# Gathering the tokens of two experts with one set of products, and moving a put into the next expert's chunks

## The chip, the cores and the metric

One core of a Trainium2 chip runs the whole program. Its engines are TensorE (PE, whose weight loads have rows of their own, PEld), VectorE (DVE), ScalarE (ACT), GpSimd (POOL) and SyncE (SP, which issues the weight transfers here). They run side by side and meet at semaphores. The metric is the device time of one execution in microseconds (us); of several runs the median counts.

## The reference

The kernel computes one inference step of a two-layer decoder for 320 tokens (a prompt of 256, and 8 sequences of 8 new tokens), 1024 features each, in float32. Each layer has a mixer (three kinds of recurrent heads) and a feed-forward part. The first layer's feed-forward part is dense. The second layer's is a mixture: a router picks 2 of 8 experts for each token, and each expert is a SwiGLU of width 1408.

```python
def moe_swiglu(h, router, wg, wu, wd):
    probs = softmax(h @ router)
    top_p, top_i = lax.top_k(probs, TOP_K)            # TOP_K = 2
    top_p = top_p / jnp.sum(top_p, axis=-1, keepdims=True)
    gates = jnp.sum(one_hot(top_i, N_EXPERTS) * top_p[..., None], axis=-2)
    out = jnp.zeros_like(h)
    for e in range(N_EXPERTS):                        # N_EXPERTS = 8
        out = out + gates[..., e:e + 1] * swiglu(h, wg[e], wu[e], wd[e])
    return out
...
def swiglu(h, wg, wu, wd):
    return (jax.nn.silu(h @ wg) * (h @ wu)) @ wd
```

After it come x += out and a final RMSNorm.

## The kernel before, in words

**Layout.** Activations are held feature by feature: `x` is 8 tiles of 128 features by 320 tokens. Each float32 operand of a large product is split into a high and a low part (`hh` and `hl`, `whi` and `wlo`), and a product is made as three: high by high, high by low, low by high.

**Weights.** All weights come as a stream of slots, each 128 x 1024 numbers (512 KB). SP loads a slot into one of 11 places of `wraw`, as soon as PE has used the slot eleven before (semaphore `slot_used`). ACT copies it, rounded, into one of 3 places of `whi` (L1196) when PE has used the slot three before; DVE subtracts to get `wlo` (L1630); then PE may use it (`slot_split`). An expert has 33 slots: 22 for gate and up, in six chunks (five of 4 slots and 512-column products, one of 2 slots and 256-column products), and 11 for down.

**One expert (layer 2, when no expert has more than 128 tokens).** The loop over the eight experts is a hardware loop (`Fori`) on each engine; the order in it is fixed by hand for each engine, and the engines wait for each other's counts.

- *Gather.* The tokens of expert i are collected by products with a 0/1 matrix: `pick` (made by DVE in `picks`, L2083) has a 1 where a token takes a place. `htk` holds the token rows, high and low part. `gather` (L1065) makes 8 feature tiles x 3 token blocks x 2 parts = 48 products of 128 columns, into banks 6 and 7 (high) and 2 and 3 (low). ACT copies the high banks into `hh` (L1526), DVE the low ones into `hl` (L2175).
- *Scales.* `slot_scales` (L1074) makes three small products that give each place its token's gate and norm factor; ACT copies them into `slot_g` (L1534).
- *Gate and up.* For each chunk PE makes 24 products (L1108 to L1110) with the places stationary and the weights moving. ACT makes `sil` (L1557), DVE `hid` (L2199), and two slots into the next chunk PE turns `hid` over (`turn`, L1092); ACT and DVE split it into `hidh` and `hidl`.
- *Placement.* `pick` is transposed by PE (L1118), and DVE copies it to `place` (L2203).
- *Down.* 66 products of 512 columns (L1129) into banks 4 and 5. ACT scales the result by the gate (`gated`, L1544), DVE makes its low part (L2192, semaphore `y_lo`).
- *Next gather.* Directly behind the last down product stand the gather and the scales of expert i + 1 (also behind expert 7, for a ninth that doesn't exist: the tables have nine columns for it).
- *Put.* 16 products of 320 columns (L1147, L1148) spread the result over the tokens, 8 feature tiles into banks 4 to 7 in turn. Even tiles go by ACT (`yt`, L1568) and POOL (L2411, x += yt); odd ones are added to `x` by DVE (L2215). Tile 4 waits for ACT's copy of tile 0 (`put_free`), tile 5 for DVE's addition of tile 1 (`dn_free`), and so on.

On DVE the order at a slot is: low part of the slot three ahead, then the chunk's `hid` if a chunk ends there, then the others. On ACT it is the high part of the slot three ahead, then silu. At slot 32 both do the part of y first.

The first gather, for expert 0, stands ahead of the loop. After the loop ACT squares `x` for the last norm (L1212), when POOL and DVE have made all their additions.

Of the kernel before, what the change touches and what calls it, by code (L numbers as in the profile page):

```python
# [22 lines left out]
F32 = mybir.dt.float32  # L23
F32R = mybir.dt.float32r
ALU = mybir.AluOpType
# [208 lines left out]
def trunk(nc, x_in, w_in, consts_in, par_in, s_rw, s_rt, s_mb, s_sh, s_cv,  # L234
# [4 lines left out]
    with ctx:  # L239
# [127 lines left out]
        pos9 = sb("pos9", [P, 3, NEXP + 1])  # L367
        rt1 = sb("rt1", [P, 3, 4])
        rs_tok = sb("rs_tok", [P, 3])
        gate_rs = sb("gate_rs", [P, 3, 2, NEXP + 1])  # L370
        slot_g = sb("slot_g", [P, 2])
# [5 lines left out]
        pick = sb("pick", [P, 3, P], F32R)  # L377
# [116 lines left out]
        def _(pe):  # L494
# [565 lines left out]
            def gather():  # L1060

                for z, bk in enumerate((6, 2)):
                    for k in range(KT):
                        for q in range(3):
                            m = mm(B[bk + k // 4][:, (k % 4) * P:(k % 4 + 1) * P], htk[z][:, q, k * P:(k + 1) * P],  # L1065
                                   pick[:, q, :], start=(q == 0), stop=(q == 2))
                    m.then_inc(S("taken"), 1)

            def slot_scales(i):

                for q in range(3):
                    of = gate_rs[:, q, :, i] if isinstance(i, int) else \
                        gate_rs[:, q, :, bass.ds(i, 1)].rearrange("p a o -> p (a o)")
                    m = mm(B[1][:, 256:258], pick[:, q, :].bitcast(F32), of,  # L1074
                           start=(q == 0), stop=(q == 2))
                m.then_inc(S("taken"), 1)

            def experts_picked():
# [3 lines left out]
                gather()  # L1082
# [12 lines left out]
                def body(i, g, e):  # L1095
                    pe.wait_ge(S("taken_hi"), 2 * i + 1)
                    pe.wait_ge(S("taken_lo"), i + 1)

                    for c, (j0, nj, nf) in enumerate(CHUNKS):
                        if c == 1:  # L1100
                            pe.wait_ge(S("taken_hi"), 2 * i + 2)
                        for j in range(j0, j0 + nj):
                            r = G_FFN[L] + j
                            pe.wait_ge(S("slot_split"), g + j + 1)
                            for kk in range(KT // nj):
                                k, cols = (j - j0) * (KT // nj) + kk, slice(kk * 2 * nf * P, (kk + 1) * 2 * nf * P)
                                out = B[c % 2][:, 0:2 * nf * P]
                                mm(out, hh[:, k, 0:P], whi[:, r % HI, cols], start=(k == 0), stop=False)  # L1108
                                mm(out, hl[:, k, 0:P], whi[:, r % HI, cols], start=False, stop=False)  # L1109
                                m = mm(out, hh[:, k, 0:P], wlo[:, POS[r], cols], start=False, stop=(k == KT - 1))  # L1110
                            m.then_inc(S("slot_used"), 1)
                            if j in TURN:
                                turn(i, TURN[j])

                    pe.wait_ge(S("put_free"), i * 4 + 4)
                    pe.wait_ge(S("dn_free"), i * 4 + KT * (1 + N_E[0]))
                    for q, (c0, n) in enumerate(BLOCKS):
                        m = pe.transpose(B[6][:, c0:c0 + n], pick[0:n, q, :].bitcast(F32),  # L1118
                                         C("ident", 0, n, slice(0, n)))
                    m.then_inc(S("place_pe"), 1)  # L1120
                    for f in range(FT):
                        if f % 2 == 0:
                            pe.wait_ge(S("hid_split"), i * NC + (N_E[0] * FT + f // 2 + 1))
                        pe.wait_ge(S("slot_split"), g + 2 * FT + f + 1)
# [9 lines left out]
                    pe.wait_ge(S("place_in"), 2 * i + 2)  # L1134
                    gather()
# [52 lines left out]
        def _(act):  # L1188
# [333 lines left out]
            def taken_hi(i):  # L1522

                act.wait_ge(S("taken"), 3 * i + 1)
                for z in range(2):
                    m = af(hh[:, 4 * z:4 * z + 4, 0:P], bank(6 + z, 4, P), ACT.Copy)  # L1526
                m.then_inc(S("taken_hi"), 1)

            def slot_scales(i):

                act.wait_ge(S("taken"), 3 * i + 3)
                if not isinstance(i, int):
                    act.wait_ge(S("y_lo"), 2 * i)
                af(slot_g[:, :], B[1][:, 256:258], ACT.Copy).then_inc(S("taken_hi"), 1)  # L1534

            def experts_picked():
# [3 lines left out]
                def gated(i, g):  # L1540

                    act.wait_ge(S("slot_used"), g + EXP_SLOTS)
                    for z in range(2):
                        af(hidh[:, 4 * z:4 * z + 4, P:2 * P], bank(4 + z, 4, P), ACT.Copy,  # L1544
                           scale=slot_g[:, 0:1]).then_inc(S("y_hi"), 1)

                def body(i, g, e):
                    for j in range(EXP_SLOTS):
                        if j == EXP_SLOTS - 1:
                            gated(i, g)  # L1550
# [989 lines left out]
```

## Time and profile before

| | |
|---|---|
| median of 3 runs | 1612.6 us (1605.84 to 1612.98) |
| the profiled execution | 1610.96 us; span in the trace 1609.2 us |
| busy over the span | PE 1449.9 us (90%), DVE 919.8 (57%), ACT 755.6 (47%), POOL 128.8 (8%) |
| mean granted clock of TensorE | 0.879 of full speed |
| weight stream | 217.61 MB over queue q1, 39.8% of the 16 DMA engines |

The span goes from the first to the last instruction of the trace. The experts run from about 1110 to 1591 us. "Granted clock" is 1.00 at 2.4 GHz and 0.50 at 1.2 GHz; a mean between them is a mixture of stretches at either level. Starts and durations of PE rows are modelled at their ends: products overlap, so the pace is read from one start to the next.

### The profile page before, as it was taken

To read this page: it belongs to the slowest core of one execution; us is meant where nothing else is said; L and a number is where in the kernel's file an instruction comes from. 1 tells how busy PE (TensorE), PEld (TensorE's weight loads), DVE (VectorE), ACT (ScalarE), POOL (GpSimd) and SP (SyncE) were. 2 spreads that over 40 slices of the span, in tenths; PEclk is the share of its full clock that TensorE was granted. 3 is DMA by queue.
4 is the path that set the end of the run, shared out by engine and by line. 5 is a ranking of instruction groups with operands and counts; after the bars stand their busy time and mean duration, and the time that the engine had idled before them with its cause. 6 is when DMAs were issued, how large, how long until landed. Compare 5 with 4: busy or idle time off the path is not lost.

```text
span 1609.2 us, 27125 instructions
## 1 busy us (share of the span) xinstructions
PE 1449.9 (90%) x10509; PEld 1253.4 (78%) x10509; DVE 919.8 (57%) x1443; ACT 755.6 (47%) x1130; POOL 128.8 (8%) x162
## 2 busy tenths in 40 slices
PE   5897889896999999889788889879999999999996
PEld 4886777766999999878667777678788778878875
DVE  4634443425554554455454343353888888988885
ACT  5521322303443243363223240344877777777784
POOL 1111011100000000001111101100000000000000
PEclk8987886856999999999778685687999999999998
DMA  5311211012554544132121110151977977977881
GB/s 222 103 63 46 67 51 58 2 51 78 199 154 132 155 146 136 49 115 79 54 73 40 42 41 8 61 204 54 326 280 278 339 277 282 340 273 273 330 291 69
DMA packets 62207, 234.93 MB, mean 146 GB/s; under 512 B 7073, under 2 KB 7169, under 8 KB 61345
## 3 DMA queue, kind: packets, MB, share of 16 engines
q1 hardware_dynamic: 59472, 217.61, 39.8%
q0 software_dynamic: 2496, 13.71, 2.3%
q10 hardware_dynamic: 144, 2.28, 0.3%
q8 instruction: 69, 1.13, 0.3%
q14 instruction: 26, 0.20, 0.0%
HBM read 225.48 MB, written 8.09 MB: 145 GB/s over the span
## 4 chain that ended last, share of the span: by engine, by line
PE 67%; issue 18%; DVE 7%; ACT 5%; POOL 1%; DMA 0%; ACTq 0%; POOLq 0%; DVEq 0%
PE bank L504 11%; PE bank L505 10%; PE bank L506 10%; PE bank L498 7%; PE bank L1129 4%; PE bank L1108 2%; PE bank L1110 2%; PE bank L1109 2%; PE bank L1065 2%; ACT whi L1196 2%; PE bank L626 1%; PE bank L520 1%; PE bank L644 1%; DVE wlo L1630 1%; PE bank L658 1%
## 5 line engine op out<-in xcount | busy, mean ns | idle before, releaser
L1630 DVE TENSOR_TENSOR wlo<-wraw,whi 128x1024 fp32r<-128x1024 f32 x410 | 506.2, 1238 | 310.4 <-ACT whi L1196 304.3
L1196 ACT ACTIVATE whi<-wraw 128x1024 fp32r<-128x1024 f32 x410 | 433.2, 1059 | 364.0 <-PE bank L506 280.0
L504 PE MATMUL bank<-hh,whi 128*128 128x320 f32 x608 | 220.2, 362 | 33.4 <-DVE hl L1654 13.8
L505 PE MATMUL bank<-hl,whi 128*128 128x320 f32 x608 | 207.8, 342 | 0.0
L506 PE MATMUL bank<-hh,wlo 128*128 128x320 f32 x608 | 206.6, 340 | 0.0
L504 PEld LDWEIGHTS bank<-hh,whi 128*128 128x128 f32 x608 | 133.3, 219 | 48.8 <-issue 31.5
L1108 PE MATMUL bank<-whi,hh 128*128 128x512 f32 (+1 forms) x384 | 149.0, 388 | 0.8 <-DVE hl L2175 0.3
L1110 PE MATMUL bank<-wlo,hh 128*128 128x512 f32 (+1 forms) x384 | 144.5, 376 | 0.0
L1109 PE MATMUL bank<-whi,hl 128*128 128x512 f32 (+1 forms) x384 | 144.1, 375 | 0.0
L505 PEld LDWEIGHTS bank<-hl,whi 128*128 128x128 f32 x608 | 133.7, 220 | 0.4
L506 PEld LDWEIGHTS bank<-hh,wlo 128*128 128x128 f32 x608 | 132.1, 217 | 0.0
L504 PE MATMUL bank<-rawh,whi 128*128 128x320 f32 x352 | 108.7, 309 | 0.0
L506 PE MATMUL bank<-rawh,wlo 128*128 128x320 f32 x352 | 108.2, 308 | 0.0
L505 PE MATMUL bank<-rawl,whi 128*128 128x320 f32 x352 | 108.2, 308 | 0.0
L1108 PEld LDWEIGHTS bank<-whi,hh 128*128 128x128 f32 x384 | 73.0, 190 | 19.5 <-DVE wlo L1630 2.8
L1110 PEld LDWEIGHTS bank<-wlo,hh 128*128 128x128 f32 x384 | 72.9, 190 | 13.7
L1109 PEld LDWEIGHTS bank<-whi,hl 128*128 128x128 f32 x384 | 73.2, 191 | 10.4
L2411 POOL TENSOR_TENSOR x<-x,yt 128x320 f32<-128x320 f32 x32 | 27.1, 881 | 508.8 <-ACT yt L1568 508.8
L504 PEld LDWEIGHTS bank<-rawh,whi 128*128 128x128 f32 x352 | 66.0, 187 | 0.2
L505 PEld LDWEIGHTS bank<-rawl,whi 128*128 128x128 f32 x352 | 66.0, 187 | 0.2
L506 PEld LDWEIGHTS bank<-rawh,wlo 128*128 128x128 f32 x352 | 66.0, 187 | 0.0
L504 PE MATMUL bank<-hidh,whi 128*128 128x320 f32 x184 | 60.2, 327 | 4.0 <-DVE hidl L2106 4.0
(388 smaller groups left out, 2454.3 us busy)
## 6 DMA issues: line engine op xcount, KB each, us to landing
wraw<-in_w SPq DMA_DIRECT2D x410, 512.0 KB, 4.9
smb<-in_s_ssm POOLq DMA_DIRECT2D x2, 1536.0 KB, 6.9
out_o_ssm<-smb POOLq DMA_DIRECT2D x2, 1536.0 KB, 5.4
cst<-in_consts ACTq DMA_DIRECT2D x1, 2225.0 KB, 13.0
srw<-in_s_rwkv POOLq DMA_DIRECT2D x2, 768.0 KB, 4.4
out_o_rwkv<-srw POOLq DMA_DIRECT2D x2, 768.0 KB, 3.6
x<-in_x SPq DMA_DIRECT2D x1, 1280.0 KB, 5.7
out_y<-x SPq DMA_DIRECT2D x2, 640.0 KB, 3.0
```

What stands on the lines that cost most here:

```text
L498: return pe.matmul(out, lhsT, rhs, start=start, stop=stop, skip_group_check=True)
L504: mm(out, hi, rh, start=first, stop=False)
L505: mm(out, hi, rl, start=False, stop=False)
L506: return mm(out, lo, rh, start=False, stop=last)
L1065: m = mm(B[bk + k // 4][:, (k % 4) * P:(k % 4 + 1) * P], htk[z][:, q, k * P:(k + 1) * P], pick[:, q, :], start=(q == 0), stop=(q == 2))
L1108: mm(out, hh[:, k, 0:P], whi[:, r % HI, cols], start=(k == 0), stop=False)
L1109: mm(out, hl[:, k, 0:P], whi[:, r % HI, cols], start=False, stop=False)
L1110: m = mm(out, hh[:, k, 0:P], wlo[:, POS[r], cols], start=False, stop=(k == KT - 1))
L1129: m = mm(B[4 + z][:, :], h_[:, f, 0:P], w_[:, z * 512:(z + 1) * 512], start=(f == 0 and q == 0), stop=(f == FT - 1 and q == 2))
L1196: af(whi[:, ring % HI, :], wraw[:, POS[ring], :], ACT.Copy).then_inc(S("slot_hi"), 1)
L1630: tt(wlo[:, POS[ring], :], wraw[:, POS[ring], :], whi[:, ring % HI, :].bitcast(F32), ALU.subtract).then_inc(S("slot_split"), 1)
L2411: tt(x[:, m_, :], x[:, m_, :], yt[:, m_ // 2, :], ALU.add).then_inc(S("yt_free"), 1)
```

## The change

One pass of the loop now holds two experts (a pair), and the last pair stands behind the loop, written out (`pairs_loop`). `pick` holds the 0/1 matrices of both experts side by side, so a gather's 48 products are 256 columns wide and serve both; the high part goes to banks 6, 7, 2, 3, the low part to 0, 1, 6, 7, bank by bank, each copied as it is done. The scales become six products into bank 0, and stand in the put (ahead of its tile 4), ahead of the loop for the first pair. The put of a pair's first expert moves behind chunk 0 of the second expert, on PE, ACT and DVE alike; that of the second stays at its end, behind the gather for the next pair. The last pair has no gather behind it. The tables lose their ninth column.

```diff
-        pick = sb("pick", [P, 3, P], F32R)
+        pick = sb("pick", [P, 3, 2, P], F32R)
...
+        def pairs_loop(eng, pair):
+            with eng.Fori(0, NEXP // 2 - 1) as p:
+                pair(p, False)
+            pair(NEXP // 2 - 1, True)
...
+            HI_BANKS, LO_BANKS = (6, 7, 2, 3), (0, 1, 6, 7)
+
+            def gather(n):
+
+                for z, banks in enumerate((HI_BANKS, LO_BANKS)):
+                    for u, bk in enumerate(banks):
+                        if z == 1 and u >= 2:
+                            pe.wait_ge(S("taken_hi"), n * 5 + (u - 1))
+                        for k in (2 * u, 2 * u + 1):
+                            for q in range(3):
+                                m = mm(B[bk][:, (k % 2) * 2 * P:(k % 2 + 1) * 2 * P], htk[z][:, q, k * P:(k + 1) * P],
+                                       pick[:, q, :, :], start=(q == 0), stop=(q == 2))
+                        m.then_inc(S("taken"), 1)
+
+            def slot_scales(p):
+
+                pe.wait_ge(S("taken_lo"), p * 4 + 1)
+                for o in range(2):
+                    for q in range(3):
+                        of = gate_rs[:, q, :, p * 2 + o] if isinstance(p, int) else \
+                            gate_rs[:, q, :, bass.ds(p * 2 + o, 1)].rearrange("p a o -> p (a o)")
+                        m = mm(B[0][:, 2 * o:2 * o + 2], pick[:, q, o, :].bitcast(F32), of,
+                               start=(q == 0), stop=(q == 2))
                 m.then_inc(S("taken"), 1)
 
...
+                def put(i, n):
+
+                    for m_ in range(KT):
+                        if m_ < 2:
+                            pe.wait_ge(S("y_lo"), i * 2 + (m_ + 1))
+                        elif m_ < 4 and n is not None:
+                            pe.wait_ge(S("taken_lo"), n * 4 + (m_ + 1))
+                        elif m_ in (4, 6):
+                            pe.wait_ge(S("put_free"), i * 4 + (m_ // 2 + 3))
+                        elif m_ in (5, 7):
+                            pe.wait_ge(S("dn_free"), i * 4 + (KT * (1 + N_E[0]) + (m_ - 3) // 2))
+                        if m_ == 4 and n is not None:
+                            slot_scales(n)
+                        mm(B[4 + m_ % 4][:, 0:T], hidh[:, m_, P:2 * P], place[:, :], start=True, stop=False)
+                        mm(B[4 + m_ % 4][:, 0:T], hidl[:, m_, P:2 * P], place[:, :], start=False, stop=True)\
+                            .then_inc(S("put"), 1)
+
+                def expert(p, o):
+                    i, g = p * 2 + o, p * (2 * EXP_SLOTS) + (o * EXP_SLOTS + G_FFN[L])
+                    ours = slice(o * P, (o + 1) * P)
                     for c, (j0, nj, nf) in enumerate(CHUNKS):
-                        if c == 1:
-                            pe.wait_ge(S("taken_hi"), 2 * i + 2)
                         for j in range(j0, j0 + nj):
                             r = G_FFN[L] + j
-                            pe.wait_ge(S("slot_split"), g + j + 1)
+                            pe.wait_ge(S("slot_split"), g + (j + 1))
                             for kk in range(KT // nj):
                                 k, cols = (j - j0) * (KT // nj) + kk, slice(kk * 2 * nf * P, (kk + 1) * 2 * nf * P)
                                 out = B[c % 2][:, 0:2 * nf * P]
-                                mm(out, hh[:, k, 0:P], whi[:, r % HI, cols], start=(k == 0), stop=False)
-                                mm(out, hl[:, k, 0:P], whi[:, r % HI, cols], start=False, stop=False)
-                                m = mm(out, hh[:, k, 0:P], wlo[:, POS[r], cols], start=False, stop=(k == KT - 1))
+                                mm(out, hh[:, k, ours], whi[:, r % HI, cols], start=(k == 0), stop=False)
+                                mm(out, hl[:, k, ours], whi[:, r % HI, cols], start=False, stop=False)
+                                m = mm(out, hh[:, k, ours], wlo[:, POS[r], cols], start=False, stop=(k == KT - 1))
                             m.then_inc(S("slot_used"), 1)
                             if j in TURN:
                                 turn(i, TURN[j])
+                        if c == 0 and o == 1:
+                            put(p * 2, None)
 
...
-                    pe.wait_ge(S("place_in"), 2 * i + 2)
-                    gather()
-                    slot_scales(i + 1)
-
-                    for m_ in range(KT):
-                        if m_ < 2:
-                            pe.wait_ge(S("y_lo"), 2 * i + m_ + 1)
-                        elif m_ == 2:
-                            pe.wait_ge(S("taken_hi"), 2 * i + 3)
-                        elif m_ in (4, 6):
-                            pe.wait_ge(S("put_free"), i * 4 + m_ // 2 + 3)
-                        elif m_ in (5, 7):
-                            pe.wait_ge(S("dn_free"), i * 4 + (KT * (1 + N_E[0]) + (m_ - 3) // 2))
-                        mm(B[4 + m_ % 4][:, 0:T], hidh[:, m_, P:2 * P], place[:, :], start=True, stop=False)
-                        mm(B[4 + m_ % 4][:, 0:T], hidl[:, m_, P:2 * P], place[:, :], start=False, stop=True)\
-                            .then_inc(S("put"), 1)
-                expert_loop(pe, L, body)
+                    pe.wait_ge(S("place_in"), p * 3 + (o + 1))
+
+                def pair(p, last):
+                    pe.wait_ge(S("taken_hi"), p * 5 + 5)
+                    pe.wait_ge(S("taken_lo"), p * 4 + 4)
+                    expert(p, 0)
+                    expert(p, 1)
+                    if not last:
+                        pe.wait_ge(S("place_in"), p * 3 + 3)
+                        gather(p + 1)
+                    put(p * 2 + 1, None if last else p + 1)
+                pairs_loop(pe, pair)
 
...
+            def taken_hi(n):
+
+                for u, bk in enumerate((6, 7, 2, 3)):
+                    act.wait_ge(S("taken"), n * 9 + (u + 1))
+                    af(hh[:, 2 * u:2 * u + 2, 0:2 * P], B[bk][:, :].rearrange("p (k c) -> p k c", k=2), ACT.Copy)\
+                        .then_inc(S("taken_hi"), 1)
+
+            def slot_scales(n):
+
+                act.wait_ge(S("taken"), n * 9 + 9)
+                af(slot_g[:, :, :].rearrange("p o a -> p (o a)"), B[0][:, 0:4], ACT.Copy).then_inc(S("taken_hi"), 1)
 
...
+                def put(i, n):
+                    for m_ in range(0, KT, 2):
+                        if m_ == 4 and n is not None:
+                            act.wait_ge(S("y_lo"), i * 2 + 2)
+                            slot_scales(n)
+                        act.wait_ge(S("put"), i * KT + (m_ + 1))
+                        act.wait_ge(S("yt_free"), i * 4 + (KT - 3 + m_ // 2))
+                        af(yt[:, m_ // 2, :], B[4 + m_ % 4][:, 0:T], ACT.Copy).then_inc(S("put_free"), 1)
+
+                def expert(p, o):
+                    i, g = p * 2 + o, p * (2 * EXP_SLOTS) + (o * EXP_SLOTS + G_FFN[L])
...
+                            if c == 0 and o == 1:
+                                put(p * 2, None)
...
+                def pair(p, last):
+                    expert(p, 0)
+                    expert(p, 1)
+                    if not last:
+                        taken_hi(p + 1)
+                    put(p * 2 + 1, None if last else p + 1)
+                pairs_loop(act, pair)
...
+            def picks(p):
+
+                for o in range(2):
+                    at = pos9[:, :, 2 * p + o:2 * p + o + 1] if isinstance(p, int) else pos9[:, :, bass.ds(p * 2 + o, 1)]
+                    m = tt(pick[:, :, o, :], rep(count_up[:, :], 3), at.to_broadcast([P, 3, P]), ALU.is_equal)
+                return m
...
+            def taken_lo(n):
+
+                for u, bk in enumerate((0, 1, 6, 7)):
+                    v.wait_ge(S("taken"), n * 9 + (u + 5))
+                    cp(hl[:, 2 * u:2 * u + 2, 0:2 * P], B[bk][:, :].rearrange("p (k c) -> p k c", k=2))\
+                        .then_inc(S("taken_lo"), 1)
...
+                def put(i):
+                    v.wait_ge(S("dn_free"), i * 4 + KT * (1 + N_E[0]))
+                    for m_ in range(1, KT, 2):
+                        v.wait_ge(S("put"), i * KT + (m_ + 1))
+                        tt(x[:, m_, :], x[:, m_, :], B[4 + m_ % 4][:, 0:T], ALU.add).then_inc(S("dn_free"), 1)
...
+                            if c == 0 and o == 1:
+                                put(p * 2)
...
-                        if j == 2 * FT + 3:
-                            picks(i + 1).then_inc(S("place_in"), 1)
+                        if j == 2 * FT + 3 and o == 1 and not last:
+                            picks(p + 1).then_inc(S("place_in"), 1)
...
+                def pair(p, last):
+                    expert(p, 0, last)
+                    expert(p, 1, last)
+                    if not last:
+                        taken_lo(p + 1)
+                    put(p * 2 + 1)
+                pairs_loop(v, pair)
 
```

## Rows read from the trace of the kernel before

**Rows 1.** Busy time by stretch, one stretch of the experts
```profile
1230.00:1290.00 60.00, 59.16 (x309) 48.51 (x308) 50.38 (x58) 46.39 (x59) 3.39 (x4) 1.00 0.83 300
```

**Rows 2.** The chain that ended last (start, us, what), one change of experts
```profile
1230.55 5.31 PE bank L1065 x48
1235.85 0.61 PE bank L1074 x6
...
1236.72 0.15 PE bank L1148
```

**Rows 3.** Timeline of the same change (start, us, engine, line, operation)
```profile
1230.38 2.79 PE L1065 MATMUL bank<-pick,htk_h 128*128 128x128 f32 x24
1230.58 1.27 ACT L1544 ACTIVATE hidh<-bank,slot_g 128x512 fp32r<-128x512 f32 x2 [0.34 <-PE bank L1129]
1231.42 1.40 DVE L2192 SCALAR_TENSOR_TENSOR hidl<-bank,slot_g,hidh 128x512 fp32r<-128x512 f32 x2
1231.74 1.06 ACT L1196 ACTIVATE whi<-wraw 128x1024 fp32r<-128x1024 f32 x1
1232.83 1.23 DVE L1630 TENSOR_TENSOR wlo<-wraw,whi 128x1024 fp32r<-128x1024 f32 x1
...
1236.99 1.60 ACT L1568 ACTIVATE yt<-bank 128x320 f32<-128x320 f32 x3 [0.23 <-PE bank L1148]
...
1237.20 2.26 DVE L2215 TENSOR_TENSOR x<-x,bank 128x320 f32<-128x320 f32 x4
...
1239.00 0.49 PE L1108 MATMUL bank<-whi,hh 128*128 128x512 f32 x1
...
1244.58 0.39 PE L1108 MATMUL bank<-whi,hh 128*128 128x512 f32 x1
```

**Rows 4.** Timeline of PE, products of 256 columns, first and last of 20
```profile
1269.82 0.28 PE L1109 MATMUL bank<-whi,hl 128*128 128x256 f32 x1
...
1272.10 0.28 PE L1110 MATMUL bank<-wlo,hh 128*128 128x256 f32 x1
```

**Rows 5.** Timeline around the first transposes of an expert
```profile
1245.86 1.28 ACT L1557 ACT_TABLE_LOAD   x1
...
1248.14 0.44 PE L1092 MATMUL bank<-cst,hid 128*128 128x128 f32 x2 [0.63 <-DVE hid L2199]
...
1249.89 0.49 PE L1108 MATMUL bank<-whi,hh 128*128 128x512 f32 x1
```

**Rows 6.** Busy time by stretch: the first gather, then the first expert
```profile
1110.00:1120.00 10.00, 9.72 (x53) 9.63 (x53) 2.87 (x9) 3.58 (x7) 0.00 (x0) 0.58 0.00 0
1120.00:1177.00 57.00, 56.16 (x270) 45.24 (x270) 46.21 (x50) 42.67 (x51) 0.00 (x0) 0.95 0.85 304
```

**Rows 7.** Timeline of PE, the first gather's second half
```profile
1112.77 5.32 PE L1065 MATMUL bank<-pick,htk_l 128*128 128x128 f32 x24
```

**Rows 8.** Timeline of the last expert's end
```profile
1580.47 2.79 PE L1065 MATMUL bank<-pick,htk_h 128*128 128x128 f32 x24
...
1587.58 3.35 POOL L2411 TENSOR_TENSOR x<-x,yt 128x320 f32<-128x320 f32 x4 [54.93 <-ACT yt L1568]
...
1591.46 0.83 ACT L1212 ACTIVATE sqb<-x 128x320 f32<-128x320 f32 x2 [2.20 <-POOL x L2411]
```

**Rows 9.** The tile pick, DVE's row (count, ns min/median/max)
```profile
L2083 DVE TENSOR_TENSOR pick<-count_up,pos x9: 550/551/557, 1106.9 to 1573.0; 128x384 fp32r<-128x384 f32 x9
```

**Rows 10.** Busy time by stretch: an idle spot in the first layer's FFN
```profile
514.30:517.70 3.40, 1.41 (x10) 1.15 (x9) 1.63 (x2) 1.42 (x2) 0.00 (x0) 1.00 0.53 154
517.70:521.10 3.40, 3.40 (x15) 3.40 (x14) 0.00 (x0) 0.00 (x0) 0.00 (x0) 0.51 0.02 5
```

**Rows 11.** The gather's line L1065: its idle time on issue (us, times)
```profile
  issue: 1.6, 1
```

**Rows 12.** DMA from 1200 to 1588 us: all its queues; weight issues to landing
```profile
q1 hardware_dynamic: 30706, 111.78, 80.7%
...
wraw<-in_w SPq DMA_DIRECT2D x211, 512.0 KB, 5.1
```

Columns of the stretches: window, its length, busy us (and instructions) of PE, PEld, DVE, ACT and POOL, granted clock, DMA share, GB/s. In a timeline the number in brackets is the engine's idle time before the row and who ended it.

More of the change, by code:

```diff
@@ L1058, in experts_dense @@
                 expert_loop(pe, L, body)
[L1060 to L1075, printed above, removed]
+            HI_BANKS, LO_BANKS = (6, 7, 2, 3), (0, 1, 6, 7)
[17 more added lines that the diff above has]
+                               start=(q == 0), stop=(q == 2))
                 m.then_inc(S("taken"), 1)
@@ L1081, in experts_picked @@
                 pe.wait_ge(S("ro_act"), 7)
-                gather()
+                gather(0)
                 pe.wait_ge(S("ro_dve"), 6)
@@ L1520, in experts_dense @@
                 act.wait_ge(S("yt_free"), KT + KT * NEXP)
[L1522 to L1534, printed above, removed]
+            def taken_hi(n):
[6 more added lines that the diff above has]
+                af(slot_g[:, :, :].rearrange("p o a -> p (o a)"), B[0][:, 0:4], ACT.Copy).then_inc(S("taken_hi"), 1)
             def experts_picked():
@@ L1553, in body @@
                             c, n = ENDS[j], CHUNKS[ENDS[j]][2] * P
-                            act.wait_ge(S("slot_used"), g + j + 1)
-                            if c == 0:
-                                act.wait_ge(S("taken_hi"), 2 * i + 2)
+                            act.wait_ge(S("slot_used"), g + (j + 1))
+                            if c == 0 and o == 0:
+                                act.wait_ge(S("taken_hi"), p * 5 + 5)
                             af(sil[:, c % 2, 0:n], B[c % 2][:, 0:n], ACT.Silu,
-                               scale=slot_g[:, 1:2]).then_inc(S("sil"), 1)
+                               scale=slot_g[:, o, 1:2]).then_inc(S("sil"), 1)
+                            if c == 0 and o == 1:
+                                put(p * 2, None)
                         if j in TURN:
                             c, n = TURN[j], CHUNKS[TURN[j]][2]
-                            act.wait_ge(S("hid_t"), i * NC + c + 1)
+                            act.wait_ge(S("hid_t"), i * NC + (c + 1))
                             af(hidh[:, 2 * c:2 * c + n, 0:P], bank(2 + c % 2, n, P), ACT.Copy).then_inc(S("hid_hi"), 1)
-                    taken_hi(i + 1)
-                    slot_scales(i + 1)
-                    for m_ in range(0, KT, 2):
-                        act.wait_ge(S("put"), i * KT + m_ + 1)
-                        act.wait_ge(S("yt_free"), i * 4 + (KT - 3 + m_ // 2))
-                        af(yt[:, m_ // 2, :], B[4 + m_ % 4][:, 0:T], ACT.Copy).then_inc(S("put_free"), 1)
-                expert_loop(act, L, body)
+                def pair(p, last):
[5 more added lines that the diff above has]
+                pairs_loop(act, pair)
                 act.wait_ge(S("yt_free"), KT + 4 * NEXP)
@@ L2078, in router @@
                 picks(0).then_inc(S("ro_dve"), 1)
-            def picks(e):
-                at = pos9[:, :, e:e + 1] if isinstance(e, int) else pos9[:, :, bass.ds(e, 1)]
-                return tt(pick[:, :, :], rep(count_up[:, :], 3), at.to_broadcast([P, 3, P]), ALU.is_equal)
+            def picks(p):
[3 more added lines that the diff above has]
+                return m
             def gates():
@@ L2169, in experts_dense @@
                 expert_loop(v, L, body)
-            def taken_lo(i):
-                v.wait_ge(S("taken"), 3 * i + 2)
-                for z in range(2):
-                    m = cp(hl[:, 4 * z:4 * z + 4, 0:P], bank(2 + z, 4, P))
-                m.then_inc(S("taken_lo"), 1)
+            def taken_lo(n):
[3 more added lines that the diff above has]
+                        .then_inc(S("taken_lo"), 1)
             def experts_picked():
@@ L2181, in experts_picked, with expert @@
                 v.wait_ge(S("ro_dve"), 5)
-                tt(gate_rs[:, :, 0, 0:NEXP], rt["g"][:, :, :], over(rs_tok[:, :], NEXP), ALU.mult)
-                cp(gate_rs[:, :, 1, 0:NEXP], over(rs_tok[:, :], NEXP)).then_inc(S("ro_dve"), 1)
+                tt(gate_rs[:, :, 0, :], rt["g"][:, :, :], over(rs_tok[:, :], NEXP), ALU.mult)
+                cp(gate_rs[:, :, 1, :], over(rs_tok[:, :], NEXP)).then_inc(S("ro_dve"), 1)
                 taken_lo(0)
                 lo(G_FFN[L] - 1 + HI, G_FFN[L] - 1 + HI)
-                def body(i, g, e):
+                def put(i):
[3 more added lines that the diff above has]
+                        tt(x[:, m_, :], x[:, m_, :], B[4 + m_ % 4][:, 0:T], ALU.add).then_inc(S("dn_free"), 1)
+                def expert(p, o, last):
+                    i, g = p * 2 + o, p * (2 * EXP_SLOTS) + (o * EXP_SLOTS + G_FFN[L])
                     for j in range(EXP_SLOTS):
@@ L2210, in body @@
                                hidh[:, 2 * c:2 * c + n, 0:P].bitcast(F32), ALU.subtract).then_inc(S("hid_split"), 1)
-                    taken_lo(i + 1)
-                    v.wait_ge(S("dn_free"), i * 4 + KT * (1 + N_E[0]))
-                    for m_ in range(1, KT, 2):
-                        v.wait_ge(S("put"), i * KT + m_ + 1)
-                        tt(x[:, m_, :], x[:, m_, :], B[4 + m_ % 4][:, 0:T], ALU.add).then_inc(S("dn_free"), 1)
-                expert_loop(v, L, body)
+                def pair(p, last):
[5 more added lines that the diff above has]
+                pairs_loop(v, pair)
             v.sem_inc(S("gu_free"), 2)
```

29 lines of the change are left out of this document (12 added, 17 removed).

## The prediction

> **What bounds the kernel now.** I read the page first (engine shares, the forty slices), then stretches, the chain, the timeline of one change of experts, the waits and the DMA view. The change touches only the experts. In a 60 us stretch of theirs, about one expert, the matrix engine (PE) is busy 59.16 us at full granted clock, VectorE (DVE) 50.38, ScalarE (ACT) 46.39, and DMA has a share of 0.83 [rows 1]. So PE sets the pace, but DVE is close behind. That decides the case: work taken from PE is worth its time only where DVE and ACT can follow.
>
> The weight path explains how close. A slot of weights costs ACT 1.06 us (high part) and DVE 1.23 us (low part), and PE about 1.37 us (24 products of 512 columns between 1239.00 and 1244.58, the first slow) [rows 3]. The high part of a slot may only start when PE has finished the slot three before it (`whi` has three buffers): 0.20 us release + 1.06 + 0.17 + 1.23 + 0.05 is about 2.7 us against two slots of PE, 2.74. The path has no slack, and whatever else ACT or DVE does shows up as a late slot, unless PE is at that moment doing something without weights. Today that something is the gather (5.31 us), the scales (0.61) and the put (sixteen products at 0.15, 2.4) [rows 2].
>
> **The price of products.** 24 gather products of 128 columns take 2.79 us with the last one's own 0.28, so 23 steps of 110 ns [rows 3]. 256-column products of the gate/up part run 1269.82 to 1272.10 in 19 steps, 120 ns each [rows 4]. So one gather of 48 products for two experts costs 5.76 us where two cost 10.62. (The Trainium skill, TensorE: Matmul & The Clock Gate, Back-to-back issue gap, gives about 81 ns for a streamed 128-column product and 109 for a lone 256-column one; by that a pair would save 48 x (2 x 81 - 109) ns = 2.5 us in place of 4.86. It speaks against the change, but this trace's 128-column products take 110, so the row decides.)
>
> The old kernel gathers nine times, the last for nobody; the new four times, wider. PE work removed: 9 x 5.31 - 4 x 5.76 = 24.8 us, and one of nine sets of scales, 0.6. This 25.4 us is what the change offers. Now what of it comes out.
>
> **Term 1, the change of experts inside a pair (four times).** No gather, scales or put stand there; the put comes after chunk 0 of the second expert. Let 0 be the moment PE ends expert 0's last slot (1230.38). ACT's gating of y lasts to 1.47 and its high part of slot 2 to 2.42; DVE's y part lasts to 2.44, its low part of slot 2 from 2.45 to 3.68 [rows 3]. That much is the trace of before, and then I carry it on with the same durations:
> PE: slot 0 at 0, slot 1 at 1.37, slot 2 ready to go at 2.74 but split only at 3.73 (stall 1.0), slot 3 at 5.10, chunk 0 done at 6.47. ACT: high parts 3 and 4 to 4.54, part 5 to 6.36 and part 6 to 7.73 (each waits for a slot of PE's), silu to about 8.1, then the `yt` copies at 0.53. DVE: low parts to 7.76, low part 6 from 7.90 to 9.13, the product `hid` to 9.55, and only then its x additions, 10.1 and 10.7 (four take 2.26) [rows 3].
> PE's put has its first four tiles out at 6.47 to 7.65 (0.295 each). Tile 4 waits for ACT's first `yt` copy (8.65), tile 5 for DVE's first x addition (10.15), 6 and 7 follow, slot 4 starts at 11.05. Unhindered it would be 6.47 + 2.36 = 8.83: a second stall of 2.2 us. What is queued behind PE here is everything: slots 4 to 6 lie split, and ACT and DVE wait for PE to use them.
> Today slot 4 starts at 1244.58, that is 14.20. Today also the first silu of each expert needs a table load of 1.28 us; `hid` comes late, PE idles 0.63 us before the transposes, and slot 7 starts at 1249.89, or 19.5 [rows 5]. In the new second expert the load should be gone (one loop pass holds both experts) and the transposes come after `hid` is long done: slot 7 at 11.05 + 4.11 + 0.44 = 15.6. Gain 3.9 us, four times: **15.6**. Bounds: with the second stall hidden 6.1 each; if the load stays and both stalls last a us longer, 1.5 each.
>
> **Term 2, between pairs (three times).** The gather is 0.45 us longer, the scales double (0.61 more), and they now stand inside the put, so a copy must not come late: the low copies end at 6.61, the put's fourth tile wants bank 7 at 6.65; scales are out at about 8.2 and copied by 8.7, before the next pair at 9.7. Loss 1.1 each: **-3.3** (bounds 0.5 and 2 each).
>
> **Term 3, the first gather.** It ran at a mean clock of 0.58 [rows 6]; its second 24 products took about 220 ns each [rows 7], twice the 110. Wider products cost some 0.9 us more there, the six extra scale products 1.4, and the pair also waits for their copy, 0.4: 2.7 us. But if the low clock ends when it did, that time would have done only half the work: **-1.3** (bounds -0.5 and -2.7).
>
> **Term 4, the end.** Without a last gather the put starts when DVE's y parts are there (1.8 and 2.5). It is stretched by the pad slot's low part (DVE, to 3.68) to 5.2, and POOL's four additions (3.35 us) end near 6.5. Today they end at 1590.93, or 10.5 after 1580.47 [rows 8]. ACT's squares begin 0.5 us after; I take 0.5 off for that restart: **+3.5** (2.5 to 5).
>
> **Term 5, picks.** Two of 0.55 us now stand together once a pair, where one stands in each expert today [rows 9]. The weight path has no slack, so the second may delay PE by its full 0.55, three times 1.65; or by nothing, since every other expert is relieved of its own. I take the middle: **-0.9** (0 to -1.7). The wider `pick`, `hh` and `hl` and the register steps cost nothing while PE has queued products to hide them. POOL's additions are unchanged and lie in the shadow of slots; if late, they hold up only a `yt` copy one expert on.
>
> **Term 6, the clock.** The first layer's FFN has an idle 2 us: PE busy 1.41 of 3.40 us, then 3.4 us at 0.51 of the clock [rows 10]. My put, from 7.65 to 11.05, has PE busy about 1.5 of 3.4 us, the same picture. It happens or not by where the stall falls; I count two falls in four at half of 3.4 us: **-3.4** (bounds 0 and -27, below).
>
> Sum: 15.6 - 3.3 - 1.3 + 3.5 - 0.9 - 3.4 = 10.2 us. The profiled execution took 1610.96 us (span 1609.2, 1.8 around it), so 1600.8; the median of the runs, 1612.6, stands 1.6 above it. I say **1602 us**, own range 1594 to 1610. What this kernel can tell from no change is about 0.5%, 8 us: its runs span 7.1.
>
> **Rivals.**
> - *The second stall hides* (0.16). If ACT and DVE reach the put in time, term 1 grows by 2.2 each and the clock does not fall: 10.2 + 8.8 + 3.4 = 22.4, **1590**. For: the clock stayed at 1.00 through today's changes of experts. Against: DVE's order is fixed, low part 6 and `hid` stand ahead of its first x addition.
> - *A fetch at each jump back* (0.12). The loop body about doubles. If it no longer stays on chip, each jump waits; the nearest row is the 1.6 us that PE idled on issue at its first gather, right after a branch [rows 11]. Two jumps and the entry of the unrolled pair, on several engines one after another, 5 us: **1607**. Against: no instruction packet in 388 us of the loop, only weights [rows 12]. (The Trainium skill, Runtime: NRT & Kernel Launch, Instruction fetch mechanics, says a taken branch outside the fetched window stalls for its page, and gives PE 2048 instructions, others 512; by my count PE's body comes to some 1,200 and the others' below 250, so it would stay.)
> - *The weights arrive late* (0.03). Two experts stream without the gather's rest, when DMA catches up. But landing takes 5.1 us [rows 12], a slot is asked for eleven slots ahead and split three ahead, eight slots of 1.4 us, so 6 us are to spare. No change or slightly slower than forecast, **1606**.
> - *The clock falls at every put and stays low longer* (0.12). At 6.8 us each the cost is 3.4 x 4 = 13.6, all of the gain: **1612**.
> - *The other side, slower* (0.07). The same fall, lasting about 14 us each as around the first gather (0.58 over 10 us, 0.95 over the next 57) [rows 6]: 4 x 7 = 28 us lost against 13.6 won, **1627**. It turns the sign once low stretches sum to 27 us, and reads slower from 43. Against: in the FFN it fell for 3.4 us only, with dense products after it, as here.
>
> My forecast has 0.50. Range for 8 in 10: **1590 to 1613**. Under 1604.5 (faster by over 0.5%): three quarters of the forecast, all of the first rival, a third of the fetch and weight cases: 0.375 + 0.16 + 0.05, so 0.59. Slower: most of the last, 0.06. Within: 0.35.
>
> **What would show it.** Gather rows: 192 products of 256 columns near 120 ns, in four groups. In the second expert of a pair: PE idle about 1 us before slot 2, released by DVE `wlo`; two idle pieces in the put, the larger released by DVE's x addition; no table load before its silu; four loads fewer. Pair period near 113 us (116.7 before). POOL's last addition about 4 us nearer to the last slot. Granted clock under 1.00 near the puts if term 6 is real. Wrong would be: a period near 110 (stalls hid), new waits on PE issue at the loop's start (fetch), or ACT waiting for DMA.

## The result and the profile after

The changed kernel takes 1584.93 us in the median (1581.09 to 1586.27, 4 runs), the kernel before in the same comparison 1609.22 (1604.42 to 1612.98, 4 runs): ratio 0.985, 95% interval 0.982 to 0.988. I forecast 10 us less and a range down to 1590; it is 24 us less. A second comparison (e5 below) gave 0.988, interval 0.986 to 0.990. The profiled execution has a span of 1584.4 us against 1609.2, 24.8 less.

The stretches of the experts in the kernel after, first gather to the end of the first expert's down part, then to the end of the second's (inside a pair), then of the third's (with the gather between), then from the last one's end. Columns as in [rows 1]:

```profile
1107.85:1165.28 57.43, 56.16 (x285) 45.85 (x285) 46.51 (x56) 44.27 (x54) 0.00 (x0) 1.00 0.78 273
1165.28:1219.70 54.42, 51.85 (x242) 40.98 (x240) 47.63 (x55) 40.88 (x51) 3.72 (x4) 1.00 0.90 323
1219.70:1279.16 59.46, 58.56 (x301) 47.99 (x300) 49.80 (x57) 45.89 (x58) 3.40 (x4) 1.00 0.81 288
1560.58:1584.40 23.82, 9.62 (x33) 5.78 (x32) 11.38 (x17) 9.42 (x17) 3.85 (x4) 0.79 0.15 58
```

The first stretch took the kernel before 62.41 us, at a mean clock of 0.89. The gather began there at full clock; 2.1 us later the clock fell to its low level (1.2 GHz) and stayed there for 13.7 us, until 6 us into the first expert:

```profile
1109.54:1171.95 62.41, 61.28 (x278) 50.29 (x279) 45.41 (x55) 43.41 (x52) 0.00 (x0) 0.89 0.71 252
1109.54:1111.64 2.10, 2.10 (x19) 2.10 (x20) 0.57 (x4) 2.09 (x3) 0.00 (x0) 1.00 0.00 0
1111.70:1125.30 13.60, 13.32 (x51) 11.98 (x51) 4.01 (x7) 4.01 (x7) 0.00 (x0) 0.50 0.11 34
```

From one down part's end to the next, every expert took the kernel before 58.3 to 58.4 us. The sum of the difference:

| place | before | after | gain |
|---|---|---|---|
| up to the first gather | 1109.54 | 1107.85 | 1.7 |
| first gather to the end of the first down part | 62.4 | 57.4 | 5.0 |
| inside a pair, four times | 58.43, 58.35, 58.35, 58.33 | 54.41, 54.40, 54.41, 54.23 | 16.0 |
| between pairs, three times | 58.36, 58.35, 58.33 | 59.47, 59.43, 58.95 | -2.8 |
| behind the last down part | 28.7 | 23.8 | 4.9 |

What stands behind the first line is no effect of the change: the kernel before, in another execution, reached its first gather at 1102.30, seven us earlier than in the profile shown, and the kernel after, in another (e5), at 1102.25.

The first gather in the kernel after, on PE's timeline, to be held against [rows 7]:

```profile
1107.85 3.11 PE L1076 MATMUL bank<-pick,htk_h 128*128 128x256 f32 x24 [1.35 <-ACT htk_l L1516]
1110.80 3.04 PE L1076 MATMUL bank<-pick,htk_l 128*128 128x256 f32 x24
```

The second 24 products take 3.04 us where they took 5.32 although they are twice as wide: PE ran at its high level (2.4 GHz) all along.

The change of experts inside a pair, from the timeline (the last down product's end, my zero, lies at 1279.16):

```profile
1280.20 1.40 DVE L2236 SCALAR_TENSOR_TENSOR hidl<-bank,slot_g,hidh 128x512 fp32r<-128x512 f32 x2
...
1282.89 0.50 PE L1135 MATMUL bank<-whi,hh 128*128 128x512 f32 x1 [0.82 <-DVE wlo L1665]
...
1287.74 0.41 PE L1121 MATMUL bank<-place,hidh 128*128 128x320 f32 x1 [0.67 <-ACT yt L1576]
...
1289.04 0.41 PE L1121 MATMUL bank<-place,hidh 128*128 128x320 f32 x1 [0.75 <-DVE x L2228]
...
1290.02 0.39 PE L1135 MATMUL bank<-whi,hh 128*128 128x512 f32 x1
```

Slot 2 starts at 3.73 after that zero, put tile 4 at 8.58, tile 5 at 9.88, slot 4 at 10.86, slot 7 at 15.21. The hand count of the prediction had 3.73, 8.65, 10.15, 11.05 and 15.6. Both stalls are there, with the releasers that were named. But the clock stays up through them:

```profile
1286.90:1290.30 3.40, 1.98 (x12) 1.52 (x11) 2.92 (x7) 1.85 (x6) 2.53 (x3) 1.00 0.69 231
```

Of the table loads, the expert stage has 6 left where it had 16: one before the high parts and one before the silu in each of three loop passes, none in the written-out pair:

```profile
L1220 ACT ACT_TABLE_LOAD x3 | 3.8, 1283 | 0.2
L1589 ACT ACT_TABLE_LOAD x3 | 3.8, 1283 | 0.1
```

In the end, ACT's squares begin at 1568.07, 7.5 us after the last down product where they began 11.0 after it [rows 8].

### The profile page after: what moved, and what is told of

It is laid out like the page before. It is cut to its first block, busy times and chain, and to the rows that moved or that the text cites. A ratio compares the mean times of both kernels' runs of the same rounds, so it can differ in the third digit from the quotient of the medians.

```text
span 1584.4 us, 26377 instructions
## 1 busy us (share of the span) xinstructions
PE 1417.6 (89%) x10263; PEld 1219.3 (77%) x10263; DVE 916.4 (58%) x1440; ACT 738.3 (47%) x1113; POOL 129.7 (8%) x162
## 4 chain that ended last, share of the span: by engine, by line
PE 54%; issue 32%; DVE 7%; ACT 5%; POOL 2%; DMA 0%; POOLq 0%; ACTq 0%; DVEq 0%
PE bank L509 11%; PE bank L510 10%; PE bank L511 10%; PE bank L503 7%; ACT whi L1220 2%; PE bank L631 1%; PE bank L525 1%; PE bank L649 1%; PE bank L663 1%; PE bank L926 1%; DVE wlo L1665 1%; PE bank L877 1%; PE bank L661 1%; PE bank L832 1%; POOL x L2459 1%
## 5 line engine op out<-in xcount | busy, mean ns | idle before, releaser
L1135 PEld LDWEIGHTS bank<-whi,hh 128*128 128x128 f32 x384 | 72.3, 188 | 20.8 <-DVE wlo L1665 7.8
```

The lines of the kernel that those rows point to most:

```text
L1135: mm(out, hh[:, k, ours], whi[:, r % HI, cols], start=(k == 0), stop=False)
```

## The experiments

Ratios are to the kernel before in the same comparison. "Stretch 1" is from the first gather to the end of the first expert's down part, "in-pair" from the end of a pair's first down part to that of its second.

**e1. The kernel before, once more.** No edit.

> The kernel before, once more, as a second look at the clock. Width theory (the 128-column products of the first gather are what lets the clock fall there): the granted clock is low again for 10 to 14 us from the first gather on, the mean clock over the span is again 0.879 within 0.002, and the first gather to the end of the first expert's last product takes 62 us again. Chance theory (where the fall lies differs from one execution to the next): this trace has no such low stretch, or one elsewhere, and the stretch takes 56 to 57 us. Time 1605 to 1613 by width, 1598 to 1613 by chance.

Measured: 1607.64 us, ratio 1.000 (0.998 to 1.001). The low clock is there again, at the same place of the program though that lay seven us earlier (the mean over the span is 0.883, more than 0.002 off 0.879, which I had not expected; other stretches differ, so that number alone is no sign). Stretch 1:

```profile
1102.30:1164.72 62.42, 61.27 (x278) 50.27 (x279) 45.41 (x55) 43.40 (x52) 0.00 (x0) 0.89 0.71 251
```

The clock falls 2.1 us behind the gather's start and stays low for 13.7 us, as in the first trace. So the fall is not chance; I had 62, and it is 62.42.

**e2. Only the first gather wide.**

```diff
+            def wide_gather():
+                for z, banks in enumerate(((6, 7, 2, 3), (0, 4, 5, 1))):
+                    for u, bk in enumerate(banks):
+                        for k in (2 * u, 2 * u + 1):
+                            for q in range(3):
+                                m = mm(B[bk][:, (k % 2) * 2 * P:(k % 2 + 1) * 2 * P], htk[z][:, q, k * P:(k + 1) * P],
+                                       pick[:, q, :, :], start=(q == 0), stop=(q == 2))
...
-                gather()
+                wide_gather()
...
+                pe.wait_ge(S("taken_hi"), 1)
```

The copies of the first gather take the 128 columns that are used from eight banks, and the scales go to bank 6.

> The kernel before with one edit: its first gather alone is made of 256-column products (the second half of the columns is not used), all else stays one expert at a time. Width theory: 0.45 us of products more, but the clock stays at 1.00 through the first gather and the first expert, so the stretch from the first gather to the end of the first expert's last product falls from 62.4 to about 57 us, and the time by 5 to 6 us, ratio 0.9965. Chance theory: no change on average, ratio 1.000, and the low stretch is there again in the trace.

Measured: 1602.71 us, ratio 0.9961 (0.9950 to 0.9973). The clock:

```profile
1105.31:1162.66 57.35, 55.55 (x278) 45.15 (x279) 45.56 (x57) 43.56 (x54) 0.00 (x0) 1.00 0.77 275
```

The stretch is 5.1 us shorter with the same number of gather products, each twice as wide, and the clock no longer falls in it. The width theory holds. This edit also uses other banks and puts the scales elsewhere; e3 comes from the other side and leaves both as they are.

**e3. The changed kernel with narrow gathers.**

```diff
-                            for q in range(3):
-                                m = mm(B[bk][:, (k % 2) * 2 * P:(k % 2 + 1) * 2 * P], htk[z][:, q, k * P:(k + 1) * P],
-                                       pick[:, q, :, :], start=(q == 0), stop=(q == 2))
+                            for o in range(2):
+                                for q in range(3):
+                                    m = mm(B[bk][:, ((k % 2) * 2 + o) * P:((k % 2) * 2 + o + 1) * P],
+                                           htk[z][:, q, k * P:(k + 1) * P], pick[:, q, o, :],
+                                           start=(q == 0), stop=(q == 2))
```

> The changed kernel with each gather made of 96 products of 128 columns in place of 48 of 256; nothing else changed. Price of the width, from 110 ns against 120 ns a product: 4.8 us more in each of four gathers, 19 us. Width theory: the low clock comes back at the first gather, 5 to 7 us on top, so 24 to 26 us over the changed kernel (ratio to before 1.000). Chance theory: 19 us alone (ratio to before about 0.997).

Measured: 1618.13 us, ratio 1.0067 (1.0050 to 1.0084), slower than the kernel before. The low clock is back, again 2.1 us behind the gather's start, and lasts 23.9 us (stretch 1, then the low part of it):

```profile
1102.25:1175.80 73.55, 72.33 (x332) 61.38 (x333) 46.49 (x56) 44.62 (x54) 0.00 (x0) 0.84 0.60 211
1104.40:1128.20 23.80, 23.36 (x101) 22.41 (x101) 4.49 (x9) 4.98 (x8) 0.00 (x0) 0.50 0.01 3
```

The stretch takes 73.55 us against 57.43, 16.1 more: 5 for the products themselves, 11 for the clock, twice what I expected. A between-pairs step is 64.4 against 59.4 us, the 5 us of the width. Three of those are 15, so 31 us in all over the changed kernel, as measured (33 against 1584.93, 31 against e5). The price of width was right, the fall of the clock right in kind and too small in size: 96 narrow products held it down for longer than 48.

**e4. The put at the end of the first expert.** `put(p * 2, None)` is called between `expert(p, 0)` and `expert(p, 1)` on PE, ACT and DVE, and no longer behind chunk 0.

> The changed kernel with the first expert's put moved back to that expert's end, ahead of chunk 0 of the second, on all engines. Stall theory of the prediction: the put waits for y and for the additions there instead, ends about 5.2 us after the last down product, and slot 4 starts at 10.7 in place of 11.05; so the same time as the changed kernel or 1 us less, ratio to it 0.999 to 1.000, and the move is worth nothing. Rival (the move is what hides the put): 2 us more at each of four places, ratio to the changed kernel 1.005.

Measured: 1587.52 us, ratio 0.9885 (0.9862 to 0.9908); e5, the changed kernel itself, has 0.9880. No difference that can be measured. In-pair steps: 55.48, 54.36, 55.46, 54.15 us against 54.41, 54.40, 54.41, 54.23. Two are the same as with the move, two are 1.1 longer, and in these the clock fell:

```profile
1159.30:1162.80 3.50, 1.73 (x7) 0.94 (x7) 3.32 (x5) 3.06 (x5) 0.00 (x0) 0.99 1.01 394
1162.80:1166.20 3.40, 3.40 (x14) 3.40 (x14) 2.31 (x4) 1.20 (x4) 2.89 (x3) 0.50 0.39 154
```

So the move by itself brings nothing but, in this execution, shelter from two such falls, about 2 us. How sparse PE was does not alone tell where the clock falls: between two other experts of the same trace it was busy for as little of as long a stretch, and the clock stayed up, there and behind it:

```profile
1273.70:1277.10 3.40, 1.73 (x9) 1.11 (x7) 3.23 (x4) 2.96 (x4) 0.00 (x0) 1.00 0.97 347
```

**e5. The changed kernel, once more.** No edit.

> The changed kernel once more, on the chip of the next three runs. Width theory: no low clock at the first gather, in this execution either; ratio to before 0.985, as measured. Its span from the first gather on is 476 to 479 us. Chance theory: the low stretch may be back. The put of a pair's first expert again has PE idle in two pieces (0.7 and 0.75 us after products that overlap) and no fall of the clock where PE is busy 2.0 of 3.4 us; with the put at the end of the expert it was 1.7 of 3.5 and fell at two of four.

Measured: 1587.02 us, ratio 0.988 (0.986 to 0.990), just above the 0.985 I expected, though the two intervals overlap. Stretch 1 again at full clock, and in-pair steps of 54.43 to 54.47 us (54.24 in the last pair):

```profile
1102.25:1159.66 57.41, 56.16 (x284) 45.86 (x285) 46.52 (x56) 44.28 (x54) 0.00 (x0) 1.00 0.75 273
```

**e6. The put's copies and additions first.**

```diff
 # ACT, slot j of expert (p, o)
+                        if j == 3 and o == 1:
+                            put(p * 2, None, (0, 2))
                         next_hi(L, i, g, j)
...
-                                put(p * 2, None)
+                                put(p * 2, None, (4, 6))
 # DVE
+                        if j == 3 and o == 1:
+                            put(p * 2, (1, 3))
                         lo(g + (j + HI), G_FFN[L] + j + HI)
...
-                                put(p * 2)
+                                put(p * 2, (5, 7))
```

> The changed kernel with another order behind chunk 0 of the second expert: ACT makes the copies of put tiles 0 and 2 before the high part of slot 6 and the silu, DVE the additions of tiles 1 and 3 before the low part of slot 6. Stall theory: the put's two waits go, slot 4 starts 9.0 in place of 11.05 us after the last down product, 2 us at four places, so 7 to 8 us less than the changed kernel (ratio to before 0.980). Rival (DVE is the bound there, and the work is only moved): slot 5, 6 or 7 comes late by as much, no change, ratio to before 0.985.

Measured: 1578.46 us, ratio 0.9828 (0.9806 to 0.9851); beside it e5 had 0.988. In-pair steps of 52.75, 52.72, 52.76 and 52.52 us, 1.7 less than e5's at each of four places, 6.8 in all. Of PE's idle time in the put hardly any is left (the put's eight tiles start from 6.6 to 8.9 us after zero), that before slot 2 stays (here zero lies at 1271.59, so slot 4 starts at 9.19, where I had 9.0):

```profile
1275.32 0.50 PE L1135 MATMUL bank<-whi,hh 128*128 128x512 f32 x1 [0.79 <-DVE wlo L1667]
...
1278.78 1.01 ACT L1576 ACTIVATE yt<-bank 128x320 f32<-128x320 f32 x2 [0.69 <-PE bank L1122]
...
1280.78 0.39 PE L1135 MATMUL bank<-whi,hh 128*128 128x512 f32 x1
```

**e7. Slot 2's parts ahead of y, inside a pair.**

```diff
 # ACT (on DVE alike: lo(...) ahead of the two y parts)
+                        if j == EXP_SLOTS - 1 and o == 0:
+                            next_hi(L, i, g, j)
+                            gated(i, g, o)
+                            continue
```

> The changed kernel with the high and the low part of slot 2 ahead of the two y parts, between a pair's two experts only. Stall theory as in the prediction (slot 2 is late because y stands ahead of it): PE's 1 us before slot 2 goes. Rival, which I hold likelier from adding up DVE's work (the low parts of slots 2 and 3 and y, 3.9 us, before slot 3 is due at 4.1): slot 3 is then late by 1.2 us, and nothing is won. Ratio to the changed kernel 0.9975 by the first, 1.000 by the rival.

Measured: 1585.05 us, ratio 0.9865 (0.9841 to 0.9888), against e5's 0.988 within both intervals; in-pair steps 54.41, 54.38, 54.39, 54.20 us, as in e5 to 0.1. The wait has moved one slot on (slot 2 starts at 1279.33, slot 3 only at 1281.58, 2.25 later):

```profile
1278.99 1.40 DVE L2242 SCALAR_TENSOR_TENSOR hidl<-bank,slot_g,hidh 128x512 fp32r<-128x512 f32 x2
...
1281.58 0.50 PE L1135 MATMUL bank<-whi,hh 128*128 128x512 f32 x1 [0.69 <-DVE wlo L1669]
```

So with the put as it stands the first stall is not one of order but of DVE's sum of work, as the rival had it.

**e8. A last gather for nobody.** All four pairs in the loop, `pos9` and `gate_rs` two columns wider.

```diff
-            with eng.Fori(0, NEXP // 2 - 1) as p:
+            with eng.Fori(0, NEXP // 2) as p:
                 pair(p, False)
-            pair(NEXP // 2 - 1, True)
```

> The changed kernel with all four pairs in the loop and so a fifth gather and set of scales, for nobody, behind the last expert. Price of the end by the prediction's hand count: the put ends later by 5.76 + 1.2 - 1.8 us, POOL's last addition 5 us later; I expect 4 to 6 us more than the changed kernel (ratio to it 1.003). Rival (the end is set by POOL and the squares, and the written-out pair costs a fetch): 0 to 2 us more.

Measured: 1591.59 us, ratio 0.9906 (0.9881 to 0.9931), 4.6 us over e5. From the last down product's start to the end of the span 29.5 against 24.3 us. The price of the end was right. This edit also puts the last pair back into the loop, and its in-pair step and the step ahead of it take 0.2 and 0.4 us more (54.45 and 59.39).

**e9 and e10. Both orders together, and the put edit once more.**

> Both edits together: put copies and additions first, and slot 2's parts ahead of y between a pair's experts. If DVE's sum of work up to slot 3 is what delays PE there, the pair of experts takes 52.7 us from down end to down end as with the put edit alone, and the ratio to before is again 0.982 to 0.983. If the order mattered, 51.7 us and 4 us less.

> The put edit alone, once more, beside the kernel with both edits: 52.7 us from the end of one down part to the next inside a pair, ratio to before 0.982 to 0.983, no low clock between the first gather and the last expert's end.

Measured: 1579.50 us, ratio 0.9825 (0.9803 to 0.9848), with both; 1578.42 us, 0.9812 (0.9788 to 0.9835), with the put edit alone; the times do not tell the two apart. The steps do: 52.45, 52.44, 52.50 and 52.23 us with both against 52.74, 52.75, 52.69 and 52.55 with the put edit alone. In e9 the put's tiles start 0.29 us apart throughout and slot 4 starts at 8.86, where e10 has 9.21. So y's order is worth 0.3 us at each of four places once the put's waits are gone, which neither expectation had; it is not the 1 us of "if the order mattered".

## Why the prediction was wrong

The direction was right, the size was not: 10.2 us were forecast, 24.8 came between the two profiled executions (24.3 between the medians, 20.8 in e5's comparison). Step by step, by its own terms.

*The price of products and the 25.4 us on offer.* Right: the wide products pace at 120 ns, e3 shows 5 us for each wide gather replaced by 96 narrow products. The Trainium skill, TensorE: Matmul & The Clock Gate, Back-to-back issue gap, gives about 81 ns for a 128-column product in a stream and about 109 ns for a lone 256-column one; the estimate from these is 2.5 us, and these runs do not agree with it.

*Term 1, the change of experts inside a pair, and term 5, the picks.* Right. Forecast 15.6 less 0.9, measured 16.0 for both. The carried-on timeline was within 0.3 us up to slot 4 and 0.4 us late at slot 7; e6 took the second stall away by the order that made it, e7 and e9 showed that the first is DVE's load. The picks cost at most the 0.2 us by which the last pair, which has none, is shorter: 0.6 in three, not the 0.9 beyond relief that I took.

*Term 2, between pairs.* Right: -3.3 forecast, -2.8 measured. The 0.5 lies in the last one, where the written-out pair has no table load; with that pair back in the loop (e8) this step takes 59.39 us like the others. I expected four loads fewer; there are ten.

*Term 3, the first gather. This is the step that failed.* I took -1.3, bounds -0.5 and -2.7, from "if the low clock ends when it did". That treated the granted clock as given, where it follows from what PE does, and so can change with the change. It was +5.0. The rows had what was needed to put a rival there: the first gather at 0.58 [rows 6], the later gathers of the same products at 1.00 [rows 1], both behind different work. I used the clock only as something that might fall at a new stall, never as something that a denser gather might lift, and none of my five rivals had it. e1 and e2 show the cause in the kernel before, one edit apart: clock 0.89 against 1.00 in stretch 1, 62.4 against 57.4 us, ratio 0.996. e3 shows the reverse in the kernel after. Against the forecast this is 6.3 us.

*Term 6, falls at the put.* Wrong in this kernel: -3.4 forecast, 0 measured in both traces of it, nor in any other trace where the put stands behind chunk 0. The kind of event is real, e4 has it twice, with the put at the end of the expert: one fell behind a stretch with PE busy 1.73 of 3.5 us, and the put of the kernel after, with 1.98 of 3.4, had none. But 1.73 of 3.40 elsewhere in e4 brought no fall, so what decides it stays open. The two falls cost 1.1 us each, not 1.7: probably part of the slow products ran where PE would have waited for DVE anyway.

*Term 4, the end.* The place was right: squares 7.5 us behind the last down product for 11.0, the forecast 3.5. Another 1.4 lie in the final norm behind it (17.7 to 16.3 us). PE's low stretches fall differently there (mean clock 0.74 from the squares on before, 0.79 after); whether that is the cause is not tested.

*What stays.* 6.3 (term 3), 3.4 (term 6), 1.4 (the norm), 1.7 (upstream, one execution against another), and 1.8 from the small misses of terms 1, 2 and 5 (1.3 and 0.5) make the 14.6 us between 10.2 and 24.8.

*The rivals.* The second stall did not hide. No fetch at a jump back: in e8, with all four pairs in the loop, only weights were moved from 1232 to 1560 us, with two jumps back in between; the only queue of that window is

```profile
q1 hardware_dynamic: 27091, 98.63, 84.1%
```

The kernel after has no instruction packet between 1232 and 1445 us either, but it has five while its written-out pair runs (1470 to 1535 us), of which three are

```profile
q8 instruction: 3, 0.05, 0.3%
```

They cost nothing that the steps show: that pair's step takes 54.23 us, the others 54.40 to 54.41. That the loop's body stays on chip agrees with the Trainium skill, Runtime: NRT & Kernel Launch, Instruction fetch mechanics, which gives PE room for 2048 instructions.

The weights were not late: inside a pair the DMA share rose to 0.90, and among the waits of the expert stage there is still none of ACT on a landing. The clock did not fall at the puts, so neither "no change" nor "slower" came.

**The better version.** The put edit of e6 beats both kernels, 0.9828 and 0.9812 in two comparisons, 8.6 us under the changed kernel beside it.

## What to carry to other kernels

Where PE sets the pace, count the work taken from it, then write the timeline of the other engines past the place where it goes, with the orders of the code: here that was right to 0.4 us and named the one reordering that paid. The granted clock is an outcome, not a given: where a stretch of the old trace ran low, ask what the edit does to PE's density there, for a gain as well as for a loss, and give both a price. Then test the price with one edit that changes that stretch alone, as e2 does. Moving a burst into another engine's queue is worth little if the order behind it is not changed too: the moved put brought nothing by itself (e4), its order 7 us (e6).

## What the runs showed that I had not expected

- A first gather of 48 products of 128 columns had the clock fall 2.1 us behind its start and stay low for 13.7 us, into the first expert, while PE was busy throughout; the same number of 256-column products in the same place kept 2.4 GHz (62.4 against 57.4 us over the stretch). With 96 narrow products it was low for 23.9 us and the stretch took 73.6.
- The same 128-column gather behind a dense down part does not lower the clock: all later ones of the kernel before ran in 5.3 us.
- Each loop pass has two table loads, one before its first high part and one before its first silu; a pair written out behind the loop has none. With four passes in place of eight the 16 loads of the expert stage became 8 (e8), with the last pair written out 6.
- Executions of the same program differ by up to 7 us in when they reach the experts (1102.30 and 1109.54 in the kernel before), while a step of the expert loop repeats within 0.1 us. Comparing steps told more than comparing times.
